# Attention's output projection in three rounded passes, its operands split in two during the attention

## The chip, the cores and the metric

One core of one Trainium2 chip runs the whole program as one launch. The metric is the device time of that launch in microseconds (us). The engines are TensorE (PE, weight loads PEld), VectorE (DVE), ScalarE (ACT), GpSimd (POOL) and SyncE (SP), which issues the large loads.

## What is computed

The reference is a two-layer diffusion block (gated linear attention, then neighbourhood attention, each with a convolutional feed-forward) followed by a second block with a mixture of experts. The change lies in the second layer's attention and the product behind it:

```python
s_nb = s_nb + bias[None]
p = softmax(concatenate([s_nb, s_cx], axis=-1))
o = einsum('bhcij,bichjd->bchd', p_nb, v_win) + einsum('bhcl,blhd->bchd', p_cx, v_c)
o_lat = o.reshape(B, N, D_MODEL) @ w_out
x_lat = x_lat + g1_l * o_lat
```

There are 256 tokens of 1024 channels, 16 heads of 64 channels, and 512 keys (256 latent, 256 context). `w_out` is 1024 x 1024. All of it is float32.

## The kernel before

The work is staged and every engine runs its own list in program order; semaphores tie the lists together. Around the change the order is: QKV products, attention, output projection, norm, feed-forward of layer 1, second block, experts.

**Split products.** Most large products round each operand to float32r (`hi`) and keep the rest (`lo` = value minus `hi`), and `split_mm` (L530) issues three matmuls, hi x hi, hi x lo and lo x hi (L532, L533, L534). ScalarE writes the `hi` parts and VectorE the `lo` parts (`w_rest`, L1793, for weights, in place over the weights in their ring slot; `h_rest`, L1798, for activations). The output projection is not done so: `project` (L568) issues one float32 matmul per pair of 128 x 128 weights and 128 x 256 inputs (L575), which the trace shows as two records.

**Attention.** The 16 heads times 2 query halves are 32 tiles, i = 0..31, taken two at a time in 16 turns, j = 0..15; `na_tile` says which head and half a tile is. Per tile: PE scores (`na_scores`, L803, into banks 4 to 7), VectorE adds the bias (`na_add`: L2038, 128x512 from a bank, then the row minimum, L2040), ScalarE `na_exp`, VectorE `na_share` (reciprocal, L2044, and a 128x512 tensor_scalar in place, L2045), PE four transposes (L840, banks 2 and 3), ScalarE copies them out. Per turn PE then multiplies by V (`na_out`, L814, banks 0 and 1 in turn), and ScalarE reads the 128x128 result (`na_read`) into `n_o`. In turn j VectorE does `na_share` for tiles 2j and 2j+1 and then `na_add` for tiles 2j+4 and 2j+5 (none in turns 14 and 15). ScalarE in turn j does the exps of tiles 2j+2 and 2j+3, the copy of tile 2j, `na_read(j-1)`, the copy of tile 2j+1. PE in turn j does the transposes of both tiles, `na_out(j-1)` and the scores of turn j+3. Transposes of tile i wait for ScalarE's copy of tile i-2, and `na_out(j-1)` for the copy of tile 2j-1.

**GpSimd** issues the bias loads (L474), one per tile into four slots: load i waits for `na_add` of tile i-4. Earlier, in the gated linear attention, it does sixteen 128x512 tensor_tensors on SBUF (L464).

**Behind the attention.** PE waits for all 16 `na_read`, and then for m = 0..7 does the 8 products of output block m in bank m % 4 and, from m = 1 on, the norm product of block m-1 (`residual_norm`, L517). That product needs ScalarE's square of the new residual, which needs VectorE's `residual` (L1777). ScalarE and VectorE first split two halves of the feed-forward's weights (`ffn_w_in_hi`, `ffn_w_in_lo` for i = 0, 1) and only then take up residual 0. SP loads two feed-forward slabs into the two `w_out` slots, after m = 3 and m = 7.

Of the kernel before, what the change touches and what calls it, by code (L numbers as in the profile page):

```python
# [7 lines left out]
F32 = mybir.dt.float32  # L8
# [3 lines left out]
ALU = mybir.AluOpType  # L12
# [108 lines left out]
def build(nc, d, out):  # L121
    ctx = ExitStack()
    with ctx:
# [106 lines left out]
        def half(w, k):  # L230

            return w[:, :, 256 * k:256 * k + 256]
# [18 lines left out]
        t = carve()  # L251
        n_q, n_k, n_v, n_bias, n_s01 = t(DC, NT), t(DC, TT), t(4, D), t(4, TT), t(2, TT)
        assert t.at[0] <= f_at
        n_o, n_pt = t(DC, NT), t(4, TT)
        t.at[0] = f_at + DC * TT
        n_s23, n_mx, n_rs = t(2, TT), t(6, 4), t(6, 4)
        assert t.at[0] <= w_at
        n_s = [n_s01[:, 0, :], n_s01[:, 1, :], n_s23[:, 0, :], n_s23[:, 1, :], sq[:, 0, :], sq[:, 1, :]]

        def na_tile(i):  # L260

            return 2 * (i // 4) + i % 2, i // 2 % 2
# [190 lines left out]
        @block.gpsimd  # L453
        def _(pool):
            for i, n in ((0, 1024), (3, 512)):
                pool.memset(ones[:, i, :], 1.0 / n).then_inc(S["ones_set"], 1)
            pool.memset(one1[:, :], 1.0).then_inc(S["ones_set"], 1)
            pool.memset(ada_sc, 0.0).then_inc(S["zeroed"], 1)
            pool.memset(eps[:, :], EPS).then_inc(S["ones_set"], 1)
            for hd in range(8):  # L460
                h, p = hd // 2, hd % 2
                for i, (x, y) in enumerate(((g_e3[:, two(h, p), :], g_qk[:, h, :]), (g_tm[:, p, :], g_qk[:, 4 + h, :]))):
                    pool.wait_ge(S["decay"], 7 * hd + 5 + i)
                    pool.tensor_tensor(x, x, y, ALU.mult).then_inc(S["late_decayed"], 1)  # L464

            pool.wait_ge(S["ffn_out_mm"], DC)
            pool.dma_start(meta, d["metaT"].rearrange("(c p) t -> p c t", p=P)).then_inc(S["meta_in"], 16)
            pool.memset(n_bias[:, :, :], 0.0).then_inc(S["zeroed"], 1)
            pool.wait_ge(S["zeroed"], 2)
            for i in range(2 * NA_H):  # L470
                if i >= 4:
                    pool.wait_ge(S["na_add"], i - 3)
                h, qt = na_tile(i)
                pool.dma_start(n_bias[:, i % 4, 0:NT], d["na_bias"][h, qt]).then_inc(S[f"na_bias_in{i % 4}"], 16)  # L474

            pool.wait_ge(S["ffn_out_mm"], 2 * DC)
            pool.dma_start(f_z[0:EMB, :], d["k_zT"]).then_inc(S["b2_in"], 16)
            pool.dma_start(f_w12[0:EMB, 0, :], d["filt_w1_2"]).then_inc(S["b2_in"], 16)
            pool.dma_start(f_w12[0:HID, 1, :], d["filt_w2_2"]).then_inc(S["b2_in"], 16)
            pool.wait_ge(S["ffn_out_x"], 3 * DC)  # L480
            pool.dma_start(q_scan, d["k_scan2"][:, 0:2 * T2]).then_inc(S["b2_in"], 16)
            pool.dma_start(q_mask, d["k_scan2"][:, 2 * T2:2 * T2 + 2 * P].rearrange("p (a n) -> p a n", n=P)).then_inc(S["b2_in"], 16)
            pool.wait_ge(S["fin_h"], DC)
            for i, (t0, n) in enumerate(TTILE):
                pool.dma_start(w_dft[0:n, i, :], d["k_dft"][t0:t0 + n, :]).then_inc(S["dft_in"], 16)
            for i in range(6):
                f0, n = FT[i % 3]
                pool.dma_start(w_inv[0:n, i, :], d["k_idft"][(i // 3) * NF + f0:(i // 3) * NF + f0 + n, :]).then_inc(S["dft_in"], 16)
            pool.wait_ge(S["mix_h"], DC)
            pool.wait_ge(S["sq_used"], norms["hyena"][0])  # L490
            for i, (t0, n) in enumerate(TTILE):
                pool.dma_start(win[i][0:n, :], d["k_win"][t0:t0 + n, :]).then_inc(S["filt_in"], 16)
            pool.wait_ge(S["hg_v_mm"], 8)
            w3 = d["filt_w3_2"].rearrange("p (r o n) -> r p o n", r=2, n=HY)
            for r in range(2):
                pool.dma_start(fw[HID * r:HID * r + HID, :, :], w3[r]).then_inc(S["filt_in"], 16)
            pool.wait_ge(S["spec_mm"], 12)
            pool.wait_ge(S["o_mm"], A_O + HEADS)
            pool.dma_start(kr, d["k_route"]).then_inc(S["route_in"], 16)
            pool.dma_start(wr, d["w_route"].rearrange("(c p) n -> p c n", p=P)).then_inc(S["route_in"], 16)  # L500
            pool.dma_start(gains, d["k_gains"]).then_inc(S["route_in"], 16)
# [3 lines left out]
        def _(pe):  # L505
            mm = pe.matmul

            def got(n):
                pe.wait_ge(S[landed[n][0]], landed[n][1])
                return place[n]  # L510
# [12 lines left out]
            def residual_norm(name, m, T):  # L523

                if m >= 1:
                    norm_chunk(name, m - 1, DC, 7, T, 1024)
                if m == DC - 1:
                    norm_chunk(name, m, DC, 7, T, 1024)
# [36 lines left out]
                        for c in range(DC):  # L565
                            mm(pb[6][:, 0:N_META], ON[1024], meta_sq[:, c, :], start=c == 0, stop=c == DC - 1)

            def project(slab, src, T, ahead, per, norm):  # L568

                for m in range(DC):  # L570
                    w = got(FIRST[slab] + m // 4)
                    if m >= 4:
                        pe.wait_ge(S["proj_x"], ahead + per * (m - 3))
                    for c in range(DC):
                        last = mm(pb[m % 4][:, 0:T], w[:, c, 128 * (m % 4):128 * (m % 4) + 128], src(c),  # L575
                                  start=c == 0, stop=c == DC - 1)
                    last.then_inc(S["proj_mm"], 1)
                    residual_norm(norm, m, T)


            def ada_products(g, bank, o):
# [224 lines left out]
            def na_out(j):  # L806
                pe.wait_ge(S["na_pt"], 2 * j + 2)
                if j >= 2:
                    pe.wait_ge(S["na_o_ev"], j - 1)
                for k in range(4):  # L810
                    for a in range(2):
                        i = 2 * j + a
                        h, qt = na_tile(i)
                        last = mm(pb[j % 2][64 * a:64 * a + 64, 0:128], n_v[:, k, 64 * h:64 * h + 64], n_pt[:, i % 4, 128 * k:128 * k + 128],  # L814
                                  start=k == 0, stop=k == 3, skip_group_check=True)
                last.then_inc(S["na_o_mm"], 1)
# [27 lines left out]
                if j + 3 < NA_H:  # L844
                    na_scores(j + 3)
            na_out(NA_H - 1)
            pe.wait_ge(S["na_o_ev"], NA_H)
            project("na_out", lambda k: n_o[:, k, :], NT, 2 * DC, 1, "n2_1")
            pe.wait_ge(S["proj_x"], 3 * DC)
            pe.wait_ge(S["rstd_ready"], norms["n2_1"][1] + 1)  # L850
            ffn(1, NT, "fin")
# [363 lines left out]
        def _(act):  # L1215
# [9 lines left out]
            def A(out, in_, func, **kw):  # L1225

                if func in TABLE_OF:
                    tables(TABLE_OF[func])
                return act.activation(out, in_, func, **kw)  # L1229
# [276 lines left out]
            def na_read(j):  # L1506
                act.wait_ge(S["na_o_mm"], j + 1)
                h, qt = na_tile(2 * j)
                A(n_o[:, h // 2, 128 * qt:128 * qt + 128], pb[j % 2][:, 0:128], ACT.Copy).then_inc(S["na_o_ev"], 1)
            for k in (10, 11):  # L1510
                half_hi(k, "na", NA_DONE)
            for u in range(8):
# [3 lines left out]
            for i in range(2 * NA_H):  # L1516
                if i % 2 == 0 and i >= 2:
                    for a in range(2):
                        if i + 2 + a < 2 * NA_H:
                            na_exp(i + 2 + a)  # L1520
                act.wait_ge(S["na_tr"], i + 1)
                if i >= 4:
                    act.wait_ge(S["na_o_mm"], i // 2 - 1)
                A(n_pt[:, i % 4, :], pb[2 + i % 2][:, :], ACT.Copy).then_inc(S["na_pt"], 1)
                if i >= 2 and i % 2 == 0:
                    na_read(i // 2 - 1)
            na_read(NA_H - 1)
            for i in range(2):
                ffn_w_in_hi(1, i)
# [213 lines left out]
        def _(dve):  # L1743
# [298 lines left out]
            def na_share(i):  # L2042
                dve.wait_ge(S["na_exp"], i + 1)
                step(dve.reciprocal(n_rs[:, i % 6, 1:2], n_rs[:, i % 6, 0:1]))  # L2044
                TS(n_s[i % 6], n_s[i % 6], n_rs[:, i % 6, 1:2], None, ALU.mult).then_inc(S["na_p"], 1)  # L2045
            for k in range(1, 11):
                half_lo(k, "na")
            for i in range(2):
# [4 lines left out]
            for j in range(NA_H):  # L2053
                for a in range(2):
                    na_share(2 * j + a)
                if j + 2 < NA_H:
                    for a in range(2):
                        na_add(2 * j + 4 + a)
            for i in range(2):
                ffn_w_in_lo(1, i)  # L2060
            for m in range(DC):
                residual(m, "proj_mm", "proj_x", m % 4, NT, 1, 2, DC)
            norm_mod("n2_1", 3, NT)
            ffn(1, NT)
            dve.wait_ge(S["ffn_out_x"], 3 * DC)
# [534 lines left out]
```

## Time and profile before

| | |
|---|---|
| median of 3 runs | 2492.93 us (2492.67 to 2493.03) |
| the profiled execution's own time | 2492.72 us |
| its span | 2490.9 us |
| PE, DVE, ACT, POOL busy | 82%, 36%, 27%, 2% |
| attention | about 917 to 977 us of the span |
| output projection | 977.8 to 1010.3 us |
| experts | from about 1560 us on, DMA busy 9 tenths or more in each slice |

Busy shares of the whole span mix stages with different limits, so the rows below come from the stages in question. A matmul record lasts longer than the distance to the next one, because matmuls are pipelined: for their rate one reads the distance of two starts.

### The profile page before, as it was taken

To read this page: it belongs to the slowest core of one execution; us is meant where nothing else is said; L and a number is where in the kernel's file an instruction comes from. 1 tells how busy PE (TensorE), PEld (TensorE's weight loads), DVE (VectorE), ACT (ScalarE), POOL (GpSimd) and SP (SyncE) were. 2 spreads that over 40 slices of the span, in tenths; PEclk is the share of its full clock that TensorE was granted. 3 is DMA by queue.
4 is the path that set the end of the run, shared out by engine and by line. 5 is a ranking of instruction groups with operands and counts; after the bars stand their busy time and mean duration, and the time that the engine had idled before them with its cause. 6 is when DMAs were issued, how large, how long until landed. Compare 5 with 4: busy or idle time off the path is not lost.

```text
span 2490.9 us, 37228 instructions
## 1 busy us (share of the span) xinstructions
PE 2046.5 (82%) x16306; PEld 1491.1 (60%) x16306; DVE 909.0 (36%) x1619; ACT 660.9 (27%) x1145; POOL 57.4 (2%) x81
## 2 busy tenths in 40 slices
PE   6998898999998998999899997766666656666665
PEld 3896555888776886898896454433344334333333
DVE  2345623343523246565566243332211111111112
ACT  4233314223424335554453201111111111111111
POOL 0010100000000011000100000000000000000000
PEclk8998999999998999999999997988888888888888
DMA  7106841222233331444530233999999999999996
GB/s 326 68 34 265 345 180 73 87 102 81 70 104 111 111 118 46 158 161 138 198 133 9 81 156 124 397 426 427 427 426 427 427 426 427 426 428 427 427 427 283
DMA packets 44432, 592.09 MB, mean 238 GB/s; under 512 B 5528, under 2 KB 5717, under 8 KB 8176
## 3 DMA queue, kind: packets, MB, share of 16 engines
q1 hardware_dynamic: 40608, 579.36, 56.9%
q0 software_dynamic: 2880, 8.45, 1.0%
q8 instruction: 130, 2.13, 0.3%
q10 hardware_dynamic: 784, 1.91, 0.2%
q14 instruction: 30, 0.25, 0.0%
HBM read 588.64 MB, written 1.05 MB: 237 GB/s over the span
## 4 chain that ended last, share of the span: by engine, by line
PE 51%; DMA 26%; DVE 5%; ACT 3%; issue 2%; SPq 0%; DVEq 0%; ACTq 0%
DMA s_ring<-in_w_up 12%; PE bank L532 10%; PE bank L534 10%; PE bank L533 10%; DMA s_arena<-in_w_up 8%; PE bank L1108 5%; DMA s_xT<-in_w_up 4%; DMA s_hT<-in_w_up 3%; PE bank L1122 2%; PE bank L1021 1%; PE bank L958 1%; PE bank L770 1%; PE bank L575 1%; PE bank L1095 1%; PE bank L758 1%
## 5 line engine op out<-in xcount | busy, mean ns | idle before, releaser
L532 PE MATMUL bank<-s_arena_r 128*128 128x256 f32 (+2 forms) x1656 | 549.0, 332 | 40.7 <-DVE s_hT_r L1798 34.0
L1229 ACT ACTIVATE s_arena<-bank 32x256 f32<-32x256 f32 (+7 forms) x439 | 173.7, 408 | 1086.1 <-PE bank L1108 573.8
L534 PE MATMUL bank<-s_arena_r,s_ring_r 128*128 128x512 f32 (+2 forms) x1312 | 443.2, 338 | 0.0
L1108 PE MATMUL bank<-s_ring,s_arena 128*32 128x256 f32 x2048 | 303.8, 511 | 133.3 <-DMA s_xT<-in_w_up 44.1
L533 PE MATMUL bank<-s_hT_r,s_arena_r 128*128 128x512 f32 (+2 forms) x1096 | 369.5, 337 | 0.0
L532 PEld LDWEIGHTS bank<-s_arena_r 128*128 128x128 f32 x1656 | 314.8, 190 | 81.3 <-issue 38.0
L1793 DVE TENSOR_TENSOR s_ring_r<-s_ring,s_arena_r 128x2048 fp32r<-128x2048 f32 (+1 forms) x96 | 232.4, 2425 | 290.0 <-ACT s_arena_r L1229 289.9
L1108 PEld LDWEIGHTS bank<-s_ring,s_arena 128*32 128x32 f32 x2048 | 150.7, 145 | 213.0 <-issue 198.9
L534 PEld LDWEIGHTS bank<-s_arena_r,s_ring_r 128*128 128x128 f32 x1312 | 251.6, 192 | 27.1
L1229 ACT ACTIVATE s_arena_r<-s_ring 128x2048 fp32r<-128x2048 f32 (+1 forms) x96 | 193.2, 2018 | 138.2 <-PE bank L534 137.0
L2370 DVE TENSOR_TENSOR s_arena<-s_arena,bank 64x256 f32<-64x256 f32 x64 | 27.1, 423 | 545.3 <-ACT s_arena L1229 545.3
L533 PEld LDWEIGHTS bank<-s_hT_r,s_arena_r 128*128 128x128 f32 x1096 | 210.8, 192 | 21.7
L1108 PE MATMUL bank<-s_arena 128*32 128x256 f32 x1024 | 129.7, 510 | 83.0 <-DMA s_arena<-in_w_up 34.8
L1108 PEld LDWEIGHTS bank<-s_arena 128*32 128x32 f32 x1024 | 64.5, 145 | 118.5 <-issue 111.8
L533 PE MATMUL bank<-s_ring_r,s_arena_r 128*128 128x256 f32 (+1 forms) x464 | 130.2, 280 | 0.0
L1229 ACT ACTIVATE s_arena<-s_arena 128x512 f32<-128x512 f32 (+8 forms) x172 | 85.4, 532 | 157.3 <-DVE s_arena L1786 77.6
L1108 PE MATMUL bank<-s_xT,s_arena 128*32 128x256 f32 x512 | 89.7, 528 | 37.4 <-DMA s_ring<-in_w_up 37.4
L533 PE MATMUL bank<-s_arena_r 128*128 128x512 f32 (+1 forms) x352 | 119.3, 339 | 0.0
L2426 DVE COPY s_arena<-bank 32x256 f32<-32x256 f32 x128 | 54.3, 424 | 143.4 <-PE bank L1122 141.0
L1108 PE MATMUL bank<-s_hT,s_arena 128*32 128x256 f32 x512 | 85.6, 508 | 18.0 <-DMA s_ring<-in_w_up 18.0
L534 PE MATMUL bank<-s_arena_r,s_hT_r 128*128 128x256 f32 (+1 forms) x336 | 94.3, 281 | 0.0
L533 PEld LDWEIGHTS bank<-s_ring_r,s_arena_r 128*128 128x128 f32 (+1 forms) x464 | 85.9, 185 | 0.5
(323 smaller groups left out, 2662.1 us busy)
## 6 DMA issues: line engine op xcount, KB each, us to landing
s_ring<-in_slabs SPq DMA_DIRECT2D x72, 2048.0 KB, 8.3
s_ring<-in_w_down SPq DMA_DIRECT2D x32, 2048.0 KB, 28.7
s_ring<-in_w_up SPq DMA_DIRECT2D x32, 2048.0 KB, 33.1
s_ring<-in_w_gate SPq DMA_DIRECT2D x32, 2048.0 KB, 33.3
s_arena<-in_w_gate SPq DMA_DIRECT2D x16, 2048.0 KB, 33.3
s_arena<-in_w_up SPq DMA_DIRECT2D x16, 2048.0 KB, 34.0
s_arena<-in_w_down SPq DMA_DIRECT2D x16, 2048.0 KB, 28.6
s_ring<-in_slabs SPq DMA_DIRECT2D x16, 1408.0 KB, 6.2
```

What stands on the lines that cost most here:

```text
L532: mm(out, w_hi_, x_hi_, start=start, stop=False)
L533: mm(out, w_hi_, x_lo_, start=False, stop=False)
L534: return mm(out, w_lo_, x_hi_, start=False, stop=stop)
L575: last = mm(pb[m % 4][:, 0:T], w[:, c, 128 * (m % 4):128 * (m % 4) + 128], src(c), start=c == 0, stop=c == DC - 1)
L758: mm(pb[m][:, :], w[:, k, 128 * (m % 4):128 * (m % 4) + 128], g_qk[:, 4 * (k % 2) + k // 2, :], start=k == 0, stop=False, skip_group_check ...
L770: last = mm(pb[m % GLA_AHEAD][:, :], w[:, k, 128 * (m % 4):128 * (m % 4) + 128], g_qk[:, 4 * (k % 2) + k // 2, :], start=k == 0, stop=k == ...
L1108: last = mm(pb[b][32 * q:32 * q + 32, 0:256], x[:, c, :], w[q // 2][:, c, 256 * (q % 2):256 * (q % 2) + 256], start=c == 0, stop=c == DC - ...
L1122: last = mm(pb[3 + b][32 * q:32 * q + 32, 0:256], e_hT[:, b, 64 * a + 32 * half_:64 * a + 32 * half_ + 32], w[:, 2 * half_ + a, 256 * q:25 ...
L1229: return act.activation(out, in_, func, **kw)
L1793: TTn(view_r, view, hi.bitcast(F32), ALU.subtract).then_inc(S["w_lo"], 1)
L2370: return TTn(e_hid[0:64, b, :], e_sg[0:64, b, :], pb[b][64:128, 0:256], ALU.mult)
L2426: dve.tensor_copy(y_g[32 * j:32 * j + 32, g % 2, 256 * q:256 * q + 256], pb[3 + b][32 * q:32 * q + 32, 0:256]).then_inc(S["y_dve"], 1)
```

## The change

`w_out` and the attention's result are split in two. `n_o` becomes `n_o_hi` (float32r, written by the same `na_read`) and `n_o_lo` (over the used-up `n_q`).

- ScalarE: `na_w_hi(q)`, eight copies of 128x1024 elements of `w_out` to float32r, one each in turns 3 to 8, right behind `na_read` and ahead of the copy of tile 2j+1, and one each in turns 13 and 14.
- GpSimd: `na_w_rest(q)`, sixteen 128x512 tensor_tensors on SBUF, one behind each bias load of tiles 14 to 25, and four behind the last load. Rest q waits for `na_w_hi(q // 2)`.
- VectorE: `na_o_rest(j)`, sixteen 128x128 tensor_tensors of a bank and `n_o_hi`; rest j-2 closes turn j, and two follow the last turn.
- PE: `na_out(j)` waits for rest j-2 and no longer for `na_read(j-2)`; the projection is `na_project`, 24 float32r matmuls per m in bank (m + 2) % 4. It waits for the results piece by piece in m = 0 (two rests ahead of each c) and no longer for all at the start.

```diff
-        n_o, n_pt = t(DC, NT), t(4, TT)
+        t.at[0] += DC * NT
+        n_pt = t(4, TT)
+        n_o_hi, n_o_lo = (arena_r[:, o:o + DC * NT].rearrange("p (c n) -> p c n", n=NT) for o in (f_at, 0))
+        hT_rflat = hT_r[:, :, :].rearrange("p a b -> p (a b)")
+        no_hi = [x.rearrange("p (c n) -> p c n", n=256) for x in (hT_rflat[:, 0:W_HALF], hT_rflat[:, W_HALF:2 * W_HALF], arena_r[:, AW - W_HALF:AW],
+                                                                  arena_r[:, DC * NT:DC * NT + W_HALF])]
+        A_NO_HI, A_NO_LO, A_NO_X = 2 * HEADS, 16, 8
...
+            def na_w_rest(q):
+                n, c = FIRST["na_out"] + q // 8, 2 * (q % 4)
+                pool.wait_ge(S["gla_y_ev"], A_NO_HI + q // 2 + 1)
+                pool.tensor_tensor(half(place_r[n], q // 4 % 2)[:, c:c + 2, :], half(place[n], q // 4 % 2)[:, c:c + 2, :],
+                                   no_hi[q // 4][:, c:c + 2, :].bitcast(F32), ALU.subtract).then_inc(S["late_decayed"], 1)
             for i in range(2 * NA_H):
                 if i >= 4:
                     pool.wait_ge(S["na_add"], i - 3)
                 h, qt = na_tile(i)
                 pool.dma_start(n_bias[:, i % 4, 0:NT], d["na_bias"][h, qt]).then_inc(S[f"na_bias_in{i % 4}"], 16)
+                if 14 <= i < 26:
+                    na_w_rest(i - 14)
+            for q in range(12, 16):
+                na_w_rest(q)
...
-            def project(slab, src, T, ahead, per, norm):
+            def na_project():
                 for m in range(DC):
-                    w = got(FIRST[slab] + m // 4)
+                    wh, wl = no_hi[m // 2], place_r[FIRST["na_out"] + m // 4]
+                    pe.wait_ge(S["late_decayed"], A_NO_LO + 4 * (m // 2 + 1))
                     if m >= 4:
-                        pe.wait_ge(S["proj_x"], ahead + per * (m - 3))
+                        pe.wait_ge(S["proj_x"], 2 * DC + m - 3)
                     for c in range(DC):
-                        last = mm(pb[m % 4][:, 0:T], w[:, c, 128 * (m % 4):128 * (m % 4) + 128], src(c),
-                                  start=c == 0, stop=c == DC - 1)
+                        if m == 0:
+                            pe.wait_ge(S["rope_s"], A_NO_X + 2 * c + 2)
+                        last = split_mm(pb[(m + 2) % 4][:, 0:NT], wh[:, c, 128 * (m % 2):128 * (m % 2) + 128], wl[:, c, 128 * (m % 4):128 * (m % 4) + 128],
+                                        n_o_hi[:, c, :], n_o_lo[:, c, :], c == 0, c == DC - 1)
                     last.then_inc(S["proj_mm"], 1)
-                    residual_norm(norm, m, T)
+                    residual_norm("n2_1", m, NT)
...
                 if j >= 2:
-                    pe.wait_ge(S["na_o_ev"], j - 1)
+                    pe.wait_ge(S["rope_s"], A_NO_X + j - 1)
...
-            pe.wait_ge(S["na_o_ev"], NA_H)
-            project("na_out", lambda k: n_o[:, k, :], NT, 2 * DC, 1, "n2_1")
+            na_project()
...
+            def na_w_hi(q):
+                n, c = FIRST["na_out"] + q // 4, 4 * (q % 2)
+                if q == 0:
+                    act.wait_ge(S["na_v_mm"], 16)
+                    act.wait_ge(S[landed[n][0]], landed[n][1])
+                if q == 4:
+                    act.wait_ge(S[landed[n][0]], landed[n][1])
+                if q == 6:
+                    act.wait_ge(S["na_s_mm"], 2 * NA_H)
+                A(no_hi[q // 2][:, c:c + 4, :], half(place[n], q // 2 % 2)[:, c:c + 4, :], ACT.Copy).then_inc(S["gla_y_ev"], 1)
...
                 if i >= 2 and i % 2 == 0:
                     na_read(i // 2 - 1)
+                if 6 <= i <= 16 and i % 2 == 0:
+                    na_w_hi(i // 2 - 3)
+                if i in (26, 28):
+                    na_w_hi(i // 2 - 7)
...
+            def na_o_rest(j):
+                dve.wait_ge(S["na_o_ev"], j + 1)
+                h, qt = na_tile(2 * j)
+                c, t0 = h // 2, 128 * qt
+                TTn(n_o_lo[:, c, t0:t0 + 128], pb[j % 2][:, 0:128], n_o_hi[:, c, t0:t0 + 128].bitcast(F32), ALU.subtract).then_inc(S["rope_s"], 1)
...
                     for a in range(2):
                         na_add(2 * j + 4 + a)
+                if j >= 2:
+                    na_o_rest(j - 2)
+            for j in range(NA_H - 2, NA_H):
+                na_o_rest(j)
             for i in range(2):
                 ffn_w_in_lo(1, i)
             for m in range(DC):
-                residual(m, "proj_mm", "proj_x", m % 4, NT, 1, 2, DC)
+                residual(m, "proj_mm", "proj_x", (m + 2) % 4, NT, 1, 2, DC)
```

## Rows read from the trace of the kernel before

**Rows 1.** Busy time by window: PE, PEld, DVE, ACT, POOL, granted clock, DMA share, GB/s

```profile
935.00:955.00 20.00, 17.35 (x144) 9.97 (x140) 19.26 (x43) 14.69 (x37) 5.91 (x11) 1.00 0.24 73
```

**Rows 2.** Line L840 (transposes): what PE sat idle for before it (us, times)

```profile
  DVE s_arena L2045: 19.5, 27
```

**Rows 3.** Timeline, VectorE in turn 13: start, us, engine, line, operation

```profile
966.21 0.49 DVE L2045 TENSOR_SCALAR s_arena<-s_arena 128x512 f32<-128x512 f32 x1
...
966.80 0.49 DVE L2045 TENSOR_SCALAR s_arena<-s_arena 128x512 f32<-128x512 f32 x1
...
967.21 0.68 DVE L2038 SCALAR_TENSOR_TENSOR s_arena<-bank,s_arena 128x512 f32<-128x512 f32 x1
...
970.03 0.49 DVE L2045 TENSOR_SCALAR s_sq<-s_sq,s_arena 128x512 f32<-128x512 f32 x1
```

**Rows 4.** Timeline of PE: float32 products (985, 989), float32r products (1021.02 to 1023.97)

```profile
985.50 3.62 PE L575 MATMUL bank<-s_arena,s_ring 128*128 128x256 f32 x16
988.95 0.59 PE L517 MATMUL bank<-s_sq,s_ones 128*128 128x256 f32 x2
989.38 3.62 PE L575 MATMUL bank<-s_arena,s_ring 128*128 128x256 f32 x16
...
1021.02 0.28 PE L534 MATMUL bank<-s_arena_r,s_ring_r 128*128 128x256 f32 x1
...
1023.97 0.28 PE L532 MATMUL bank<-s_arena_r 128*128 128x256 f32 x1
```

**Rows 5.** Timeline, end of the attention and start of the projection

```profile
973.80 0.63 PE L840 MATMUL bank<-s_ka,s_arena 128*128 128x128 f32 x4 [0.37 <-ACT s_arena L1229]
...
976.32 1.09 PE L814 MATMUL bank<-s_arena 128*64 128x128 f32 x16 [0.87 <-ACT s_arena L1229]
...
977.79 7.17 PE L575 MATMUL bank<-s_arena,s_ring 128*128 128x256 f32 x32 [0.38 <-ACT s_arena L1229]
979.57 4.49 DVE L1793 TENSOR_TENSOR s_ring_r<-s_ring,s_arena_r 128x2048 fp32r<-128x2048 f32 x2 [7.27 <-ACT s_arena_r L1229]
...
984.96 0.70 PE L517 MATMUL bank<-s_sq,s_ones 128*128 128x256 f32 x2
```

**Rows 6.** Groups by line and shape, VectorE: busy us, mean ns, idle before

```profile
L2116 DVE TENSOR_SCALAR s_arena<-s_arena 128x272 f32<-128x272 f32 x8 | 2.4, 302 | 0.3
...
L2174 DVE COPY s_arena<-bank 128x128 f32<-128x128 f32 x4 | 1.1, 285 | 12.9 <-PE bank L921 12.9
```

**Rows 7.** Groups by line and shape, ScalarE: the 128x1024 SBUF to SBUF form

```profile
L1229 ACT ACTIVATE s_arena<-s_arena 128x1024 f32<-128x1024 f32 x2 | 2.1, 1056 | 1.6 <-DVE s_arena L2375 1.6
```

**Rows 8.** Timeline, PE and ScalarE in turns 13 and 14

```profile
967.93 1.10 PE L814 MATMUL bank<-s_arena 128*64 128x128 f32 x16
...
969.07 0.77 ACT L1229 ACTIVATE s_arena<-bank 128x128 f32<-128x128 f32 x2 [1.03 <-PE bank L814]
...
971.27 0.60 ACT L1229 ACTIVATE s_arena<-bank 128x512 f32<-128x512 f32 x1
```

**Rows 9.** Line L464, GpSimd tensor_tensors: duration min/median/max, starts

```profile
L464 POOL TENSOR_TENSOR s_arena<-s_arena x16: 1260/1398/1862, 166.2 to 305.9; 128x512 f32<-128x512 f32 x16
```

**Rows 10.** Timeline of GpSimd in the attention: a bias load's issue

```profile
960.53 0.54 POOL L474 DMA_DIRECT2D s_arena<-in_na_bias  x1 [1.97 <-DVE s_arena L2038]
```

**Rows 11.** Timeline of GpSimd in the gated linear attention

```profile
166.17 3.56 POOL L464 TENSOR_TENSOR s_arena<-s_arena 128x512 f32<-128x512 f32 x2 [164.67 <-ACT s_arena L1229]
```

**Rows 12.** Timeline of VectorE at the same time, operands all in SBUF

```profile
166.98 1.59 DVE L1921 TENSOR_TENSOR s_arena<-s_arena 128x512 f32<-128x512 f32 x1
...
170.31 0.69 DVE L1923 TENSOR_TENSOR s_arena<-s_arena 128x512 f32<-128x512 f32 x1
```

**Rows 13.** Timelines, same stage: GpSimd, and a VectorE instruction with a bank operand

```profile
211.19 3.08 POOL L464 TENSOR_TENSOR s_arena<-s_arena 128x512 f32<-128x512 f32 x2 [30.88 <-ACT s_arena L1229]
...
211.38 0.73 DVE L1947 COPY_PREDICATED s_arena<-s_ka,bank 128x512 f32<-128x512 uint32 x1
```

**Rows 14.** Busy time by window, columns as in rows 1: PE behind the norm

```profile
1015.00:1021.00 6.00, 6.00 (x29) 6.00 (x30) 3.06 (x7) 5.98 (x12) 0.00 (x0) 0.51 0.04 16
```

More of the change, by code:

```diff
@@ L1508, in na_read @@
                 h, qt = na_tile(2 * j)
-                A(n_o[:, h // 2, 128 * qt:128 * qt + 128], pb[j % 2][:, 0:128], ACT.Copy).then_inc(S["na_o_ev"], 1)
+                A(n_o_hi[:, h // 2, 128 * qt:128 * qt + 128], pb[j % 2][:, 0:128], ACT.Copy).then_inc(S["na_o_ev"], 1)
+            def na_w_hi(q):
[8 more added lines that the diff above has]
+                A(no_hi[q // 2][:, c:c + 4, :], half(place[n], q // 2 % 2)[:, c:c + 4, :], ACT.Copy).then_inc(S["gla_y_ev"], 1)
             for k in (10, 11):
```

## The prediction

> **What bounds the kernel now.** The windows come first. In the attention's steady part VectorE is busy 19.26 of 20.00 us, PE 17.35 and ScalarE 14.69, at a granted clock of 1.00, TensorE's 2.4 GHz [rows 1]. The waits of the transposes say the same from PE's side: 19.5 us of idle time before them ended with VectorE's scaling, L2045 [rows 2]. The timeline of VectorE in turn 13 shows one turn: 966.21 to 970.03, 3.82 us from one L2045 to the same one of the next turn [rows 3]. Instruction follows instruction there, so whatever is put on VectorE in turns 2 to 13 is paid in full. In turns 14 and 15 it has no `na_add`, and the chain through PE and ScalarE decides. In the projection PE decides: a block m costs it 989.38 - 985.50 = 3.88 us, of which the 8 float32 products take 988.95 - 985.50 = 3.45 and the norm product 0.43 [rows 4]. Behind it the stages follow in series, so what is won or lost here should reach the end one for one.
>
> **Projection: what it gains.** The float32r rate stands in the feed-forward behind: 26 matmuls of the same form start from 1021.02 to 1023.97, 25 distances of 0.118 us [rows 4]. 24 of them take 2.83 us in place of 3.45, so a block gains 0.62. Not all eight blocks count. In front of block 2 stands the norm product of block 0. It started at 984.96, because VectorE was held by two weight rests (979.57, 4.49 us) ahead of residual 0 [rows 5]. Those hang on ScalarE's reads and copies, which stay the same distance behind the last `na_out`; the faster blocks 0 and 1 end about 1.9 us earlier and PE then waits for it. The cover is gone there, the gain is nothing, and the 0.38 us that PE waited at 977.79 for the last read is lost in the same wait. Blocks 2 to 7 count: 6 x 0.62 = **-3.7**. Bounds: -5.0 if all eight counted, -3.3 if two blocks' worth of small waits came back (0.2 each).
>
> **VectorE's result rests.** 12 of the 16 (rests 0 to 11) fall into turns 2 to 13. The nearest row is the 128x128 copy from a bank, 285 ns [rows 6]; VectorE's next start comes about 0.08 earlier than the end (L2045: 0.49 long, next start 0.41 on [rows 3]), so 0.20 each: **+2.4**. Bounds 0.15 and 0.29: +1.8 and +3.4. The other four lie beside PE's and ScalarE's work. PE's new wait (rest j-2 for `na_out(j)`) is met a turn ahead. Rest 15 is due only at c = 7 of block 0.
>
> **ScalarE's weight copies.** The 128x1024 form takes 1.06 us [rows 7]. In turns 3 to 8 each delays the copy of the turn's second tile and everything behind it on ScalarE. ScalarE waits 1.03 us per turn for `na_out` [rows 8], the exps run a turn ahead, and the first user, the next turn's second transpose, wants it later: the copy of tile 27 would end near 970.9 (969.07 + 0.17 + 1.06 + 0.60), and that transpose needs the second scaling of turn 14, done at 966.80 + 3.82 + 0.20 + 0.49 = 971.3 [rows 3, 8]. So the six hide, barely; if not, up to 0.3 us each. In turns 13 and 14 there is no such cover: there the chain is `na_out`, read, copy of tile 29, transpose 31 (PE waited 0.37 for it), `na_out(14)`, last `na_out` at 976.32 [rows 5]. The copy of turn 14 lies in it in full: **+1.0**.
>
> **GpSimd's weight rests.** A 128x512 tensor_tensor takes at least 1.26 us there [rows 9], a bias issue 0.54 [rows 10]; two of each are 3.6 us in a turn of 4, and a load issued a turn late still has a turn to land. That queue costs nothing by itself. What it does to VectorE is the question. In the earlier stage GpSimd's pair of tensor_tensors took 3.56 us from 166.17 on [rows 11], and the VectorE tensor_tensor that came upon it took 1.59 us, while the next free one took 0.69: 0.90 longer [rows 12]. The two wait for each other, one whole instruction at a time. An instruction with one operand in a bank ran unstretched (0.73) while GpSimd worked [rows 13]. So `na_add` and the result rests should be free of it. The scaling L2045 is one SBUF input, and no row shows such a one beside GpSimd: bounds 0 (as with the bank operand) and 1.1 (GpSimd's whole instruction less its end). Which is it like? It handles 512 elements in 0.49 us, where a tensor_tensor takes 0.69, and the same kind takes 0.30 for 272 [rows 3, 6, 12]: it moves data faster than one SBUF stream of the others, so I hold that it takes the same doors as a two-input instruction, and take 0.95.
>
> The page "SBUF — State Buffer" of the Trainium skill (section "Who interferes with whom") has the rule that the row leaves open: a tensor_scalar on SBUF can run in a two-port mode, and then it and a GpSimd instruction exclude each other for a whole instruction. By it the sum is the one below; without it, it is rival B.
>
> **How often.** Rest q waits for `na_w_hi`. In turn 13's clock that copy would end 3.5 us behind the start of the turn's second scaling (966.80; read at 969.07 [rows 3, 8], the copy then from about 969.24 to 970.30), and GpSimd wants to start at 3.6. The next turn's first scaling starts at 970.03 + 0.20, that is 3.4, and runs to 3.9. So GpSimd comes in behind it, and the second scaling, due at 4.0, waits until about 4.9. The other rest of the turn then runs beside `na_add`. This repeats, since `na_out`, read and copy all follow the delayed scaling: once per turn, six turns, 6 x 0.95 = **+5.7**. The last four rests add one more on the chain of turns 14 and 15: **+1.0**.
>
> **Sum.** -3.7 + 2.4 + 1.0 + 5.7 + 1.0 = **+6.4 us**. The profiled execution took 2492.72, 0.2 below the median, and the sum is made against it: 2499.1; against the median 2499.3, which I forecast.
>
> **The rivals.**
> - A, the forecast: one collision per turn, +6.4. For it: rows 9 to 13 and the phases above. Against it: no row shows L2045 beside GpSimd. 0.50.
> - B, the other side, not slower: GpSimd does not stop the scaling, because it has one SBUF input only, or the phases miss. Both +5.7 and +1.0 fall: -3.7 + 2.4 + 1.0 = -0.3 us, 2492.6. It decides where the collisions cost less than 0.6 us a turn; from there on the loss stays under 5 us. 0.22.
> - C: both rests of a turn hit a scaling. GpSimd needs 3.6 us a turn, so a small shift brings the second rest there too: 6 more x 0.95, +12.1, 2505.0. 0.13.
> - D: the clock. PE waits longer in the attention and 1.9 us in the projection. Behind the norm, where PE had stood still for over 4 us, 6 us went at a granted 0.51, its 1.2 GHz level, at twice the distance per matmul [rows 14], which is 3 us lost. One such stretch in or ahead of the projection gives +9.4, 2502.3. Against it: the attention already has waits of 0.5 us at each turn at 1.00. 0.12.
> - E: the rests hide and the copy of turn 14 too, because another wait sets the turn: -3.7 + 1 = -2.7, 2490.2. Little for it, VectorE has no gap. 0.03.
>
> That the change does not do what it says is no rival of weight: the three passes and their splits are all in the diff.
>
> **The numbers.** 0.2% of 2492.93 is 5.0 us, about what a measurement of this kernel tells from no change. A lies on the slower side in some 0.38 of its 0.50: a collision may cost 0.7 instead of 0.95, which takes 1.7 off. C and D are slower; B is the same. Slower 0.62, same 0.35, faster 0.03. The range goes from B's value with its bounds (2492.0) to C's with its bounds (2505.5).
>
> **What would show it.** Right: L2045 at 0.49 outside turns 4 to 9 and about 1.4 for one of the two in them; turns of about 4.0 and 5.0 us; the tensor_tensors of GpSimd at 1.3 to 1.8 us; blocks 2 to 7 of the projection at 3.27 us, and a wait of some 1.9 us in front of the first norm product; a last `na_out` some 10 us later than 976.32. Wrong: L2045 unstretched throughout (B), both stretched (C), a PEclk below 1.00 between 917 and 1010 us (D), or ScalarE's copies as what ends PE's waits in turns 4 to 9.

## The result

The changed kernel took 2501.41 us (median of 6 runs, 2498.9 to 2501.9) against 2492.45 before (6 runs, 2486.36 to 2493.03): ratio 1.0039, 95% interval 1.0027 to 1.0051, so 7 to 13 us slower. Taken again beside other kernels (x11) it gave 2499.21 against 2492.16, ratio 1.0021 (1.0010 to 1.0033), so 2 to 8 us slower. The forecast was 2499.3, +6.4 us. Single runs of one kernel spread by several us, so the stage itself is measured inside the traces, by two distances that don't depend on what came earlier:

- **A**, from the issue of the bias load of tile 8 on GpSimd to the start of the last attention output product.
- **B**, from there to the start of the norm's logarithm on ScalarE, behind block 7.

| us | A | B | A + B | span |
|---|---|---|---|---|
| before | 57.84 | 34.03 | 91.87 | 2490.9 |
| changed | 68.24 | 30.38 | 98.62 | 2497.0 |

The stage is 6.75 us longer: +10.40 in the attention, -3.65 in the projection. The span grew by 6.1 us. The changed trace reached tile 8's load 3.2 us sooner (915.30 for 918.48), with nothing changed ahead of it, and lost 2.5 us behind the stage. Both are no larger than what two profiles of one kernel differ by: the second profile of the changed kernel (x11) reached that load at 918.57, and behind the stage it took 1479.6 us, where the first took 1483.1 and the kernel before 1480.6. The projection's gain does reach the next stage whole: the feed-forward's first matmul starts 38.47 us behind the last output product before and 34.83 us in the changed kernel.

### The profile page after: what moved, and what is told of

The parts are those of the page before. It is cut to its first block, busy times and chain, and to the rows that moved or that the text cites. A ratio compares the mean times of both kernels' runs of the same rounds, so it can differ in the third digit from the quotient of the medians.

```text
span 2497.0 us, 37397 instructions
## 1 busy us (share of the span) xinstructions
PE 2044.3 (82%) x16370; PEld 1489.2 (60%) x16370; DVE 918.7 (37%) x1635; ACT 667.7 (27%) x1153; POOL 78.8 (3%) x97
## 3 DMA queue, kind: packets, MB, share of 16 engines
HBM read 588.64 MB, written 1.05 MB: 236 GB/s over the span
## 4 chain that ended last, share of the span: by engine, by line
PE 51%; DMA 27%; DVE 5%; ACT 3%; issue 2%; DVEq 0%; ACTq 0%
DMA s_ring<-in_w_up 13%; PE bank L549 10%; PE bank L550 10%; PE bank L551 10%; DMA s_arena<-in_w_up 6%; PE bank L1126 5%; DMA s_xT<-in_w_up 5%; DMA s_hT<-in_w_up 3%; PE bank L1140 2%; PE bank L1039 1%; PE bank L976 1%; PE bank L789 1%; PE bank L1146 1%; ACT s_arena_r L1247 1%; PE bank L777 1%
## 5 line engine op out<-in xcount | busy, mean ns | idle before, releaser
L549 PE MATMUL bank<-s_arena_r 128*128 128x256 f32 (+2 forms) x1688 | 558.9, 331 | 40.8 <-DVE s_hT_r L1832 33.9
L551 PE MATMUL bank<-s_arena_r,s_ring_r 128*128 128x512 f32 (+2 forms) x1376 | 460.8, 335 | 0.0
L1247 ACT ACTIVATE s_arena<-bank 32x256 f32<-32x256 f32 (+8 forms) x423 | 170.9, 413 | 1072.0 <-PE bank L1126 573.6
L549 PEld LDWEIGHTS bank<-s_arena_r 128*128 128x128 f32 x1688 | 320.5, 190 | 81.1 <-issue 38.2
L551 PEld LDWEIGHTS bank<-s_arena_r,s_ring_r 128*128 128x128 f32 x1376 | 263.7, 192 | 27.2
L1247 ACT ACTIVATE s_arena_r<-s_ring 128x2048 fp32r<-128x2048 f32 (+2 forms) x100 | 197.3, 1978 | 138.2 <-PE bank L551 137.0
L550 PE MATMUL bank<-s_arena_r 128*128 128x256 f32 (+1 forms) x384 | 128.3, 334 | 0.0
L1247 ACT ACTIVATE s_arena<-bank,s_cols 128x512 f32<-128x512 f32 (+2 forms) x76 | 48.6, 649 | 141.6 <-PE bank L551 115.7
```

Of the source, the lines that this page charges most:

```text
L549: mm(out, w_hi_, x_hi_, start=start, stop=False)
L550: mm(out, w_hi_, x_lo_, start=False, stop=False)
L551: return mm(out, w_lo_, x_hi_, start=False, stop=stop)
```

## The profile after

VectorE in turn 4 and at the start of turn 5 of the changed kernel, from the timeline (start, us, engine, line, operation); L2079 is the scaling, L2085 the result rest:

```profile
929.02 0.49 DVE L2079 TENSOR_SCALAR s_arena<-s_arena 128x512 f32<-128x512 f32 x1
929.42 0.16 DVE L2078 RECIPROCAL s_arena<-s_arena 128x1 f32<-128x1 f32 x1
929.61 1.31 DVE L2079 TENSOR_SCALAR s_arena<-s_arena 128x512 f32<-128x512 f32 x1
930.84 0.68 DVE L2072 SCALAR_TENSOR_TENSOR s_arena<-bank,s_arena 128x512 f32<-128x512 f32 x1
931.55 0.69 DVE L2074 TENSOR_REDUCE s_arena<-s_arena 128x1 f32<-128x512 f32 x1
...
933.48 0.28 DVE L2085 TENSOR_TENSOR s_arena_r<-bank,s_arena_r 128x128 fp32r<-128x128 f32 x1
...
933.86 0.49 DVE L2079 TENSOR_SCALAR s_sq<-s_sq,s_arena 128x512 f32<-128x512 f32 x1
...
934.45 1.30 DVE L2079 TENSOR_SCALAR s_sq<-s_sq,s_arena 128x512 f32<-128x512 f32 x1
```

GpSimd at the same time; L481 is the weight rest, L487 the bias load:

```profile
929.17 1.47 POOL L481 TENSOR_TENSOR s_ring_r<-s_ring,s_hT_r 128x512 fp32r<-128x512 f32 x1 [1.66 <-ACT s_hT_r L1247]
930.58 0.55 POOL L487 DMA_DIRECT2D s_arena<-in_na_bias  x1
931.16 1.29 POOL L481 TENSOR_TENSOR s_ring_r<-s_ring,s_hT_r 128x512 fp32r<-128x512 f32 x1
...
934.01 1.46 POOL L481 TENSOR_TENSOR s_ring_r<-s_ring,s_hT_r 128x512 fp32r<-128x512 f32 x1 [1.08 <-ACT s_hT_r L1247]
```

[rows 3] has both scalings at 0.49. Here the second takes 1.31: it should have run from 929.61 to 930.10 and ended at 930.92, 0.82 later. GpSimd's rest starts at 929.17, 0.15 us into the first scaling, waits for its end, and runs for about 1.26 of its 1.47 (two in a row without a wait take 2.51, below). The second scaling gets in when it is over. Beside GpSimd's other rest (931.16) `na_add` and the row minimum take their usual 0.68 and 0.69. Turn 4 lasts 933.86 - 929.02 = 4.84 us. All 32 scalings in one view, by tile (duration ns min/median/max):

```profile
L2079 DVE TENSOR_SCALAR s_arena<-s_arena x22: 485/487/1310, 893.3 to 977.6; 128x512 f32<-128x512 f32 x22
L2079 DVE TENSOR_SCALAR s_sq<-s_sq,s_arena x10: 485/486/1310, 921.0 to 974.7; 128x512 f32<-128x512 f32 x10
```

The window over the steady part, columns as in [rows 1], and windows over turns 14 and 15:

```profile
935.00:955.00 20.00, 13.64 (x113) 7.97 (x112) 19.44 (x37) 15.04 (x36) 15.59 (x18) 1.00 0.18 54
970.00:974.00 4.00, 2.27 (x24) 1.69 (x24) 3.86 (x11) 2.75 (x7) 0.00 (x0) 1.00 0.01 2
977.00:980.00 3.00, 2.75 (x21) 2.04 (x20) 1.31 (x4) 0.83 (x2) 0.17 (x1) 0.64 0.00 0
980.00:984.00 4.00, 2.12 (x28) 1.73 (x30) 0.29 (x1) 2.13 (x5) 2.50 (x2) 1.00 0.03 6
```

PE's busy time fell from 17.35 to 13.64 in 20 us, VectorE stayed full. The clock, which was 1.00 throughout this stretch before, fell to 0.64 in the window 977 to 980. In windows of 1 us it reads 0.50 from 976 to 979, TensorE's 1.2 GHz, and 0.89 and 0.91 in the two beside them, which is about 3.4 us at half clock. That shows in PE's timeline (L859 transposes, L833 output products, L534 norm products):

```profile
974.69 0.66 PE L859 MATMUL bank<-s_ka,s_sq 128*128 128x128 f32 x4 [1.75 <-DVE s_sq L2079]
976.10 1.11 PE L859 MATMUL bank<-s_ka,s_sq 128*128 128x128 f32 x4 [0.76 <-DVE s_sq L2079]
977.14 1.98 PE L833 MATMUL bank<-s_arena 128*64 128x128 f32 x16
...
983.54 1.09 PE L833 MATMUL bank<-s_arena 128*64 128x128 f32 x16 [0.86 <-ACT s_arena L1247]
...
992.18 0.70 PE L534 MATMUL bank<-s_sq,s_ones 128*128 128x256 f32 x2 [1.66 <-ACT s_sq L1247]
```

The output product at 977.14 took 1.98 us, the others 1.09, and the transposes at 976.10 took 1.11 for 0.66. In front of them PE had waited 1.75 and 0.76 us. The norm product of block 0 stands 992.18 - 983.54 = 8.64 us behind the last output product, exactly as before (984.96 - 976.32 [rows 5]), and PE waited 1.66 us for it.

## The experiments

Each is an edit of the changed kernel unless it says otherwise. The values of A and B come from one profile of each, the ratios from timed runs in turn with the kernel before.

| | A | B | A + B | ratio to before (95%) |
|---|---|---|---|---|
| x1 no weight rests | 61.17 | 30.36 | 91.53 | 0.9988 (0.9977 to 1.0000) |
| x2 rests timed | 62.39 | 30.35 | 92.74 | 0.9993 (0.9983 to 1.0004) |
| x3 no result rests | 65.64 | 30.40 | 96.04 | 1.0017 (1.0005 to 1.0029) |
| x4 copies 6, 7 late | 66.22 | 30.39 | 96.61 | 1.0014 (1.0004 to 1.0023) |
| x7 residual 0 first | 66.91 | 29.85 | 96.76 | 1.0025 (1.0013 to 1.0037) |
| x8 memsets | 62.15 | 30.35 | 92.50 | one run, 2492.62 us |
| x10 splits between residuals | 66.87 | 28.44 | 95.31 | one run, 2493.28 us |
| x11 changed again | 68.26 | 30.38 | 98.64 | 1.0021 (1.0010 to 1.0033) |
| x5 x2 + x4 + x7 | 60.24 | 29.87 | 90.11 | 0.9988 (0.9979 to 0.9997) |
| x6 x5 + result rests later | 58.71 | 29.87 | 88.58 | 0.9984 (0.9975 to 0.9992) |
| x9 x6 + x10's order | 58.69 | 28.43 | 87.12 | 0.9978 (0.9969 to 0.9988) |

### Does GpSimd stretch the scaling? (x1, x2, x8)

x1:

```diff
-                pool.tensor_tensor(half(place_r[n], ...)[:, c:c + 2, :], half(place[n], ...)[:, c:c + 2, :], no_hi[q // 4][...], ALU.subtract).then_inc(S["late_decayed"], 1)
+                pool.sem_inc(S["late_decayed"], 1)
```

> The changed kernel without GpSimd's sixteen tensor_tensors on the weights (its semaphore counts stay, and the third pass of the projection reads the high part of the weights in place of the rests, so the projection's result is another). Measures: A is the stretch from the issue of the bias load of tile 8 to the start of the last attention output product (57.84 us before, 68.24 changed), B from there to the norm's logarithm (34.03 and 30.38). Theory of the port (GpSimd and VectorE's scaling shut each other out): every scaling takes 0.49, turns 3 to 9 take 4.02 instead of 4.84, and the tail loses its two collisions; A falls by 6 x 0.83 + 0.83 + 0.62 = 6.4 to about 61.8, B stays. Rival (ScalarE's copies in the attention lengthen the turns): A stays near 68. Time against before: port theory about +0.5 us, rival about +7.

A fell by 7.1 to 61.17; every one of the 32 scalings took 0.485 to 0.490. The rival is out: the six copies on ScalarE are in this kernel too, and they don't lengthen the turns. The split of the 7.1 is not the expected one, though. 1.35 is the clock, which no term of the expectation held: all of x1's output products took 1.09, while the changed profile has one at 1.98 (below). The six collisions are 4.9, and 0.8 is left for the end of the attention, where 1.45 was expected.

x2 keeps all the work and moves it in time:

```diff
             for i in range(2 * NA_H):
+                if 16 <= i < 28 and i % 2 == 0:
+                    pool.wait_ge(S["na_p"], i - 6)
+                    for q in range(2):
+                        na_w_rest(i - 16 + q)
                 if i >= 4:
                     pool.wait_ge(S["na_add"], i - 3)
...
-                if 14 <= i < 26:
-                    na_w_rest(i - 14)
+            pool.wait_ge(S["na_p"], 2 * NA_H)
             for q in range(12, 16):
                 na_w_rest(q)
```

> All the work of the changed kernel, but GpSimd starts its rests behind the second scaling of a turn (two rests, then the turn's two bias loads), the last four behind the last scaling. Port theory: the two rests (2.6 us) fit between the second scaling and the next turn's first (3.0 us later), no scaling is stretched, A falls to about 61.8 as without them, time about +0.5 us against before. Rival (GpSimd's traffic slows VectorE or the bias loads in any phase): turns of 4.0 stay out of reach, A stays above 65.

No scaling above 0.490. GpSimd and VectorE (scalings alone) in two turns of x2:

```profile
937.97 2.51 POOL L481 TENSOR_TENSOR s_ring_r<-s_ring,s_hT_r 128x512 fp32r<-128x512 f32 x2 [0.48 <-DVE s_sq L2082]
...
940.42 1.09 POOL L491 DMA_DIRECT2D s_arena<-in_na_bias  x2
```

```profile
936.80 0.49 DVE L2082 TENSOR_SCALAR s_sq<-s_sq,s_arena 128x512 f32<-128x512 f32 x1
...
937.40 0.49 DVE L2082 TENSOR_SCALAR s_sq<-s_sq,s_arena 128x512 f32<-128x512 f32 x1
...
940.83 0.49 DVE L2082 TENSOR_SCALAR s_arena<-s_arena 128x512 f32<-128x512 f32 x1
```

The pair of rests starts 0.08 us behind the end of the second scaling (937.40 + 0.49) and ends at 940.48, 0.35 before the next turn's first scaling. The turn is 940.83 - 936.80 = 4.03 us. The same twelve rests cost the steady turns 4.9 us in one phase and nothing in the other. A is 62.39, 0.6 above the expected and 1.22 above x1's, whose turns are as long as these: here too the clock fell in turn 14 (granted 0.55 in the window 974 to 977, one output product at 1.98).

x8 asks which side of GpSimd's instruction does it:

```diff
-                pool.tensor_tensor(...).then_inc(S["late_decayed"], 1)
+                pool.memset(half(place[n], q // 4 % 2)[:, c:c + 2, :], 0.0).then_inc(S["late_decayed"], 1)
```

> The changed kernel with each GpSimd tensor_tensor replaced by a memset of the same 128x512 elements at the same place (the third pass reads the high part of the weights, so the projection's result is another): GpSimd writes SBUF but reads none of it. If the scaling is shut out by GpSimd's reads alone, every scaling takes 0.49 and A is about 61.2, as in x1. If the write side shuts it out as well, the scaling that comes upon a memset (which should take 0.4 to 0.6 us) is longer by up to 0.4, and A lies at 62 to 64.

```profile
932.18 0.82 POOL L481 MEMSET s_ring<- 128x512 f32 x1 [1.63 <-ACT s_hT_r L1246]
...
933.48 0.54 POOL L481 MEMSET s_ring<- 128x512 f32 x1
```

```profile
932.06 0.49 DVE L2078 TENSOR_SCALAR s_arena<-s_arena 128x512 f32<-128x512 f32 x1
...
932.65 0.63 DVE L2078 TENSOR_SCALAR s_arena<-s_arena 128x512 f32<-128x512 f32 x1
```

The memset, 0.54 us alone, starts 0.12 into the first scaling (932.06) and takes 0.82. The second scaling takes 0.63 for 0.49. An instruction that only writes SBUF shuts the scaling out as well, and for as long as it lasts: the last 0.49 us of the stretched scaling begin at 932.79, 0.21 ahead of the memset's recorded end (933.00), and in the changed kernel at 930.43, again 0.21 ahead of the rest's (930.64). By the page "SBUF — State Buffer" of the Trainium skill (section "Who interferes with whom") a two-port instruction takes the shared pair, read and write, and a two-input one only its read side. The trace agrees for the scaling (0.63 for 0.49); no run here puts a two-input instruction beside a memset.

### Is VectorE's turn the bound? (x3)

```diff
-                TTn(n_o_lo[:, c, t0:t0 + 128], pb[j % 2][:, 0:128], n_o_hi[:, c, t0:t0 + 128].bitcast(F32), ALU.subtract).then_inc(S["rope_s"], 1)
+                dve.sem_inc(S["rope_s"], 1)
```

> The changed kernel without VectorE's sixteen result rests (the semaphore counts stay; the second pass reads the high part of the results in place of the rests, so the result is another). If VectorE sets the turn: turns of 3.82 and 4.64 us instead of 4.02 and 4.84, A lower by 12 x 0.20 = 2.4, to about 65.9, with the collisions still there unless the 0.20 shifts GpSimd's start into another phase: it wants to start 3.6 us behind the second scaling, and the next first scaling then runs from 3.2 to 3.7, so the second scaling is still the one hit. Rival (the rests hide beside PE's work): A stays at 68.

The turns were 4.65 and 3.82 us, A 65.64: 2.6 lower. The same scalings were hit (1.30 or 1.31 each). So each of the twelve rests in turns 2 to 13 costs its full 0.20, 2.4 us, and hides beside nothing; the last 0.2 comes from the end of the attention.

### The end of the attention (x4)

```diff
-                if i in (26, 28):
-                    na_w_hi(i // 2 - 7)
             na_read(NA_H - 1)
             for i in range(2):
                 ffn_w_in_hi(1, i)
+            for q in (6, 7):
+                na_w_hi(q)
```

> The copies 6 and 7 of the weights moved on ScalarE from turns 13 and 14 behind the feed-forward's two weight copies, after the attention; GpSimd's last four rests follow them. Theory: the tail loses one copy (1.0) and its two collisions (0.83 and, beside the copy, 0.4 to 0.6): A falls by 1.8 to 2.4, to about 66.1; B stays at 30.4, since the rests for blocks 4 to 7 have over 10 us. Rival (the tail's chain runs past the copy): A stays at 68.2.

66.22, as expected, and B did not move: the last four blocks' weights are split in time during the projection. This profile has an output product at 1.98 too, so its 66.22 compares with the changed kernel's 68.24: of the 2.0 us the copy is 0.9 (x1, below), and most of the rest goes with the two collisions of turns 14 and 15, 1.31 and 1.11 for 0.49 in the changed kernel; here all four scalings of the last two turns take 0.48 or 0.49.

The clock is a term of its own. Two kernels with the same attention as the changed one, x7 and x10, kept 1.00 there: A = 66.91 and 66.87, no output product above 1.09. The changed kernel and x11 had one product at 1.98 and A = 68.24 and 68.26. PE of x7, at the place where the changed kernel has its lines 976.10 and 977.14:

```profile
979.74 0.66 PE L859 MATMUL bank<-s_ka,s_sq 128*128 128x128 f32 x4 [0.76 <-DVE s_sq L2081]
980.33 1.09 PE L833 MATMUL bank<-s_arena 128*64 128x128 f32 x16
```

The starts of the transposes and of the next product lie 0.59 us apart here and 1.04 there, and the product is 0.89 longer there. So the half clock costs this attention 1.35 us when it comes. It cost x2 1.22 (62.39 against x1's 61.17) and x4, by an estimate, 1.06 (66.22 against x5's 60.24 and six collisions of 0.82). With the clock held the attention is 9.05 us longer: 12 x 0.20 = 2.4, 6 x 0.82 = 4.9, and 1.75 in turns 14 and 15, of which 0.9 is the copy (x1: 61.17 - 57.84 - 2.4) and 0.8 what the last rests do. (The difference to x4 would give them 1.1; the half clock cost 0.3 less there.)

### The wait in front of block 0's norm product (x7, x10)

x7 (ScalarE's squares and copies in the same way: square 0 and 1 ahead of the first copy):

```diff
-            for i in range(2):
-                ffn_w_in_lo(1, i)
             for m in range(DC):
                 residual(m, "proj_mm", "proj_x", (m + 2) % 4, NT, 1, 2, DC)
+                if m in (1, 2):
+                    ffn_w_in_lo(1, m - 1)
```

> The changed kernel with one thing moved: residual and square of block 0 ahead of the feed-forward's first weight splits. Theory (PE's wait of 1.66 us in front of block 0's norm product hangs on those splits alone): A stays at 68.2, B falls by 1.7 to 1.9, from 30.4 to 28.6, and the pitch of all blocks is 3.27. Rival (the wait hangs on the last read, or the splits then delay the feed-forward's start): B plus the time to the feed-forward's first matmul (4.45) stays at 34.8.

Half of it missed. Block 0's norm product came at 6.81 us instead of 8.64, but B fell by 0.5 only. VectorE and PE's norm products of x7:

```profile
995.63 2.29 DVE L1829 TENSOR_TENSOR s_ring_r<-s_ring,s_arena_r 128x2048 fp32r<-128x2048 f32 x1 [2.29 <-ACT s_arena_r L1247]
997.84 0.48 DVE L1813 SCALAR_TENSOR_TENSOR s_xT<-bank,s_mod,s_xT 128x256 f32<-128x256 f32 x1
1000.60 2.29 DVE L1829 TENSOR_TENSOR s_ring_r<-s_ring,s_arena_r 128x2048 fp32r<-128x2048 f32 x1 [2.29 <-ACT s_arena_r L1247]
1002.81 0.87 DVE L1813 SCALAR_TENSOR_TENSOR s_xT<-bank,s_mod,s_xT 128x256 f32<-128x256 f32 x2
```

```profile
999.21 0.59 PE L534 MATMUL bank<-s_sq,s_ones 128*128 128x256 f32 x2
1003.79 0.70 PE L534 MATMUL bank<-s_sq,s_ones 128*128 128x256 f32 x2 [1.17 <-ACT s_sq L1247]
```

The wait had moved. ScalarE made each copy only behind a square, VectorE's rest waited for it, and residuals 2 and 3 stood behind the rests (997.84, 1002.81); PE then waited 1.17 us for block 3's square. x10 leaves ScalarE alone and interleaves on VectorE with `if m < 2: ffn_w_in_lo(1, m)`:

> The changed kernel with that order on VectorE alone (residual 0, rest 0, residual 1, rest 1, residual 2): ScalarE's squares stay behind its two weight copies, which end 5.0 us after the last output product. Theory: block 0's norm product at 6.8 instead of 8.64 us, no other wait, B = 28.5 to 28.6, and so the forecast that the first two blocks' gain is lost in that wait alone is shown. Rival: B at 29.9 or above.

```profile
991.57 2.28 DVE L1827 TENSOR_TENSOR s_ring_r<-s_ring,s_arena_r 128x2048 fp32r<-128x2048 f32 x1
994.01 0.48 DVE L1811 SCALAR_TENSOR_TENSOR s_xT<-bank,s_mod,s_xT 128x256 f32<-128x256 f32 x1 [0.17 <-PE bank L551]
994.41 2.28 DVE L1827 TENSOR_TENSOR s_ring_r<-s_ring,s_arena_r 128x2048 fp32r<-128x2048 f32 x1
997.29 0.48 DVE L1811 SCALAR_TENSOR_TENSOR s_xT<-bank,s_mod,s_xT 128x256 f32<-128x256 f32 x1 [0.60 <-PE bank L551]
1000.57 0.48 DVE L1811 SCALAR_TENSOR_TENSOR s_xT<-bank,s_mod,s_xT 128x256 f32<-128x256 f32 x1 [2.79 <-PE bank L551]
```

```profile
986.98 1.09 PE L833 MATMUL bank<-s_arena 128*64 128x128 f32 x16 [0.86 <-ACT s_arena L1247]
993.81 0.59 PE L534 MATMUL bank<-s_sq,s_ones 128*128 128x256 f32 x2
997.09 0.59 PE L534 MATMUL bank<-s_sq,s_ones 128*128 128x256 f32 x2
```

PE waits for no square but that of block 7, the last, where it waits in every profile. The residuals of blocks 1 to 3 come at 994.01, 997.29, 1000.57, a rest fits between two, and B = 28.44. So the two early blocks' gain was lost in that wait alone, 1.9 us. Nor is it paid back behind: the feed-forward's first matmul starts 32.88 us behind the last output product, 1.95 sooner than in the changed kernel.

### A faster kernel (x5, x6, x9) and the changed one again (x11)

x5 is x2 with three more moves: copies 6 and 7 right behind the last read of the attention; ScalarE's two feed-forward copies behind squares 1 and 2; VectorE's two feed-forward rests behind residuals 1 and 2, as in x7:

> All the work, in three changed places: GpSimd's rests timed as in x2, copies 6 and 7 behind the attention as in x4, and the residual and square of block 0 (and 1) ahead of the feed-forward's first two weight splits, which follow blocks 1 and 2. By the terms found so far: A falls to 57.84 + 12 x 0.20 = 60.2 (x1's 61.2 less the copy); B to 30.4 - 1.9 = 28.5, since PE no longer waits for block 0's norm product. A + B = 88.7 against 91.87 before: 3.2 us faster than before, ratio 0.9987. Rival (the last copies and the splits behind the attention delay a square or a block): B stays above 30, no gain over before.

A was right to 0.04 us. B, expected at 28.5, was 29.87, for x7's reason. x6 takes the result rests out of the turns (PE's waits follow, not shown):

```diff
+                A(n_q[:, h // 2, 128 * qt:128 * qt + 128], pb[j % 2][:, 0:128], ACT.Copy).then_inc(S["na_o_ev"], 1)
                 A(n_o_hi[:, h // 2, 128 * qt:128 * qt + 128], pb[j % 2][:, 0:128], ACT.Copy).then_inc(S["na_o_ev"], 1)
...
-                if j >= 2:
-                    na_o_rest(j - 2)
-            for j in range(NA_H - 2, NA_H):
-                na_o_rest(j)
+            for c in range(DC):
+                dve.wait_ge(S["na_o_ev"], 4 * c + 4)
+                TTn(n_o_lo[:, c, :], n_q[:, c, :], n_o_hi[:, c, :].bitcast(F32), ALU.subtract).then_inc(S["rope_s"], 1)
```

> As x5, and VectorE's sixteen result rests leave the attention: ScalarE writes the result a second time in float32 (0.17 us more in each turn, in its idle time), and VectorE does eight 128x256 rests behind the last scaling. Theory (VectorE sets the turn): turns of 3.82, A = 57.9 to 58.3 (0.2 to 0.4 from the last read), B 28.5 or up to 0.5 more, A + B = 86.6 against 91.87 before: 5.3 us faster, ratio 0.998. Rival (ScalarE, with two exps, two copies, two reads and a weight copy of 1.05 in a turn, becomes the bound of turns 3 to 8): those turns stay at 4.0, A at 59.1 or more.

A = 58.71, 0.4 above the expected, and B was again 29.87 and not 28.5 to 29.0, so A + B came to 88.58 for 86.6. The turns with rests are 3.91 instead of 3.82, because in each of the six the first scaling takes 0.57 to 0.59. It starts 0.15 us behind the end of GpSimd's pair of rests and beside the issue of a bias load; which of the two does it was not tried (in x2 such an issue beside a scaling left it at 0.49). ScalarE is full there but not late. x9 adds x10's order (ScalarE's two feed-forward copies right behind the last read, copies 6 and 7 behind squares 1 and 2):

> As x6, but the feed-forward's first two weight copies stay right behind the last read on ScalarE, and VectorE takes residual 0, rest 0, residual 1, rest 1, residual 2. In x5 to x7 block 0's norm product came 1.83 us earlier, but residual 3 stood behind the second rest and PE waited 1.16 us for its square. Theory: without that wait B falls from 29.87 to 28.5 to 28.7; A stays at x6's 58.7; A + B = 87.3 against 91.87 before, 4.6 us faster, ratio 0.998. Rival (a later square is late in turn): B stays at 29.9.

A + B = 87.12, 4.75 us below the kernel before, and the time says the same: 2486.18 against 2492.16 us, ratio 0.9978 (0.9969 to 0.9988), so 3 to 8 us less. In the same timing the changed kernel took 2499.21 (x11), so x9 is faster than both.

> The changed kernel itself, on the chip of the best version: A 68.2 (66.9 if the clock holds in turns 14 and 15), B 30.4, and about 8 us slower than before.

A and B repeat to 0.02 us, with the half clock again. It is 7.1 us slower than before in the median, where about 8 was expected.

## Why the prediction was right

- **Projection, -3.7.** Measured -3.65: norm products 3.27 to 3.29 us apart instead of 3.88 or 3.89 (the first distance 3.38 instead of 3.99), the float32r matmuls 0.118 apart, blocks 0 and 1 worth nothing behind the wait for residual 0. x10 shows the lost 1.9.
- **Result rests, +2.4.** 0.20 each in twelve turns: turns without a collision are 4.02, and 3.82 without the rest (x3).
- **Collisions in the steady turns, +5.7.** Six, at the place foretold (the second scaling of turns 4 to 9), each 0.82 and not 0.95: +4.9. The scaling was due at 929.61 and started about 930.43, 0.49 ahead of its end, while GpSimd's rest is recorded to end at 930.64. The unknown, whether a one-input scaling is like a bank operand or like a two-input instruction, was settled on the right side by its speed per element. That argument held but was not itself tested: no run changes the scaling's speed, and x8 shows that GpSimd's writes alone stop the scaling too, which the prediction did not ask. The odds of 0.22 that it is free of GpSimd fell to nothing with the first profile.
- **ScalarE's six copies, nothing.** They hide, as forecast: x1 keeps them and its turns are 4.02.
- **Turns 14 and 15, +2.0.** 1.75 with the clock held: 0.9 for the copy, and 0.8 for the last rests, which hit two scalings (1.31 and 1.11) and not one. In the changed profile it is 3.1. The difference is the price that was missed: 3.4 us of half clock at the end of the attention, worth 1.35. Rival D had it in or ahead of the projection, at 3 us and 0.12, and its sign, a clock below 1.00 between 917 and 1010 us, was met together with A's: what came is A with a smaller D on top.
- **Sum.** +6.4 forecast, +6.75 in the changed trace, +5.4 with the clock held (66.89 + 30.38 - 91.87). By terms: 6.4, less 0.8 for the collisions and 0.25 for turns 14 and 15, plus 1.35 for the clock and 0.05 for the projection, is 6.75. The mechanisms are the ones forecast, but that the sum comes so close is luck: the clock, in no term, makes up for terms that were 1.05 too large. The first timing's +9.0 is above the stage's own difference, and the second timing's +7.1 is close to it; what the first adds was not traced.
- **Rival C** (both rests collide) did not come: the second rest ran beside `na_add` in every turn. **Rival E** fell with x3.

## What to carry to other kernels

Work given to GpSimd does not always run beside VectorE's. Here `na_add` and the row minimum kept their time, but a scaling from SBUF to SBUF that met one of GpSimd's instructions waited for its end (0.82 us), and the phase decided whether they met, so tie GpSimd's start to the end of the instruction it must not meet. On an engine without a gap, as VectorE here, even 0.2 us per turn is paid in full; put behind the loop (x6), it gave back 1.5 of the 2.4 us. And before counting a faster product, look at what stands next to it in program order: a residual behind two weight splits swallowed two blocks' gain, and moving it well meant placing the splits between residuals, not merely behind them.

## What was not expected of the hardware

- GpSimd's memset, which reads no SBUF, stretched a scaling by 0.14 us (x8).
- The granted clock fell to half in turn 14 for 3.4 us although PE had not stood still for longer than 1.75 us. It did so in the profiles of the changed kernel and x11 (waits of 1.75 and 0.76 us), x3 (1.55 and 0.76), x2 (1.75 alone) and x4 (1.74 alone), one output product at 1.98 each, and in none of the others. x7 and x10, whose instructions there are those of the changed kernel, kept 1.00 behind the same two waits, and x1 behind 1.75 alone. What tips it was not tried.
